# The order of scores, projections and transposes on TensorE in the attention of a hybrid decoder layer

## The chip, the cores and the metric

One NeuronCore of a Trainium2 chip runs the whole layer as one program. The time is that of one execution on the device, in microseconds (us); the kernel before took 1571.97 us, the median of 3 runs from 1569.59 to 1573.26. TensorE multiplies matrices into PSUM, VectorE (DVE), ScalarE (ACT) and GpSimd (POOL) work on tiles, SyncE issues most of the DMAs. Each engine works through its own list of instructions in program order, and semaphores tie the lists together.

## The reference, cut to what matters

One layer for 1024 tokens and a width of 1024: an input projection feeds two kinds of attention, their outputs are gated, merged and projected, and a SwiGLU feed-forward part follows.

```python
qa, ka, va, qb, kb, vb, f_logit, gate_logit = jnp.split(h @ w_in, IN_OFFSETS, axis=-1)

# branch A: 8 query heads, 2 key heads, rotary, a window of 128 keys, a sink per head
s = where(valid, einsum('bnqhgd,bnkhd->bnhgqk', qb_, kb_) * scale, -inf)
p = exp(s - m) / (sum(exp(s - m)) + exp(sink - m));  o_a = p @ v

# branch B: 8 heads, causal over all keys, with the sum of log forget gates
s = einsum('bqhd,bkhd->bhqk', qi, k) * scale + ci - cum_k
p = softmax(where(causal, s, -inf));                 o_b = p @ v

merged = gates[0] * (o_a @ w_branch_a) + gates[1] * (o_b @ w_branch_b)
y = merged @ w_out;  x = x + gate_m * rms_norm(y)
x = x + gate_f * rms_norm((silu(g_part) * u_part) @ w_ffn_out)
```

## The kernel before, in words

Every fp32 product is made of three TensorE products of high and low halves (`TERMS`: hi x hi, hi x lo, lo x hi), so each projection of 512 columns takes 3 x 8 = 24 matmuls, and every operand is split into two halves first.

The attention is one loop of numbered steps (`for gp in range(FIRST, NG)`), written out for each engine separately; the same step numbers run through all of them. Branch A has 16 tiles of 4 heads x 128 queries and takes steps 0 to 31, two groups for each tile. Branch B works on four pairs of heads; the pair `pb` starts at step b = `step0(pb)` = 32, 56, 80, 104 and has 24 groups. Its scores come in eight rows: row r holds 128 queries against (r + 1) x 128 keys for two heads. Steps around the change:

- `scores(r)` on TensorE writes the scores to PSUM. Rows 4 to 7 of a pair use all of the banks 0 to 3, so each waits until DVE has taken the row before (`s_taken`). Which step issues a row stands in `issue_step`: for pairs 2 to 4 rows 0 to 3 in b-11, b-9, b-7, b-5 and rows 4 to 7 in b+1 to b+4; for pair 1 rows 0 to 3 in 25, 27, 27, 28.
- `score_stat(r)` on DVE (L1174 for branch B) adds the forget bias, takes the maximum and writes the row to SBUF (`s_row`). It stands last in DVE's step; in the following step `exps_b` on ACT (L832) makes the exponentials, and two steps after the statistic `denominator` on DVE (L1188) the reciprocal and `normalise` on GpSimd (L674) the probabilities.
- `transpose_p(gp + 1)` on TensorE (L1618, L1624) transposes the 128 x 128 tiles of the next group into bank 4 or 5. It waits for the normalised rows (`norm_ok`) and for the low half of two groups back (`grp_lo`). `group_hi` on ACT (L843) and `group_lo` on DVE (L1193) make the two halves, `group_lo` as the first thing in DVE's step.
- `times_v(gp)` (L1651, L1652) multiplies group gp with the values. The first group of an output waits until DVE has added up the output before (L1200 to L1204).
- `project(j, first, end)` (L1545) makes pieces of the projections that the next pair needs, 4 or 5 matmuls a step in branch B (8 in steps 25 and 27). `fills` says which steps carry which chunk. The second chunk of a pair (steps b+5 to b+10) writes bank 1, so its first piece waits until all eight rows of the pair are taken. In the last pair the pieces belong to the gates, and this chunk starts at b+6.

The loop on TensorE:

```python
            for gp in range(FIRST, NG):
                between = 0 <= gp < 2 * A_T and gp % 2 == 0
                for r in range(N_S):
                    if issue_step[r] == gp and not between:
                        scores(r)
                for j, first, end in mm_at[gp]:
                    project(j, first, end)
                if 0 <= gp + 1 < NG:
                    transpose_p(gp + 1)
                for r in range(N_S):
                    if issue_step[r] == gp and between:
                        scores(r)
                if gp >= 0:
                    times_v(gp)
```

Of the kernel before, what the change touches and what calls it, by code (L numbers as in the profile page):

```python
# [39 lines left out]
def hybrid_layer(nc, x, c, positions, w_ada, b_ada, g_pre_mix, g_post_mix, w_in, b_f, sinks,  # L40
# [165 lines left out]
    A_T, B_P = 2 * NTOK, 4  # L206
    NG = 2 * A_T + B_P * 3 * NTOK
# [25 lines left out]
    def banks(r):  # L233
        is_a, _, i = score_parts(r)
        if is_a:
            return [PS[:, 2 * (r % 2) + kv] for kv in range(2)]
        if i < 4:
            return [PS[:, 2 * (i % 2) + h] for h in range(2)]
        return [PS[:, 2 * h:2 * h + 2].rearrange("p a n -> p (a n)") for h in range(2)]
# [8 lines left out]
    def group_cols(gp):  # L248
        is_a, _, g, _, kb = group_parts(gp)
        if is_a:  # L250
            return 2 * P if g == 0 else NT
        return P * (4 * g + 4 - max(4 * g, kb))
# [100 lines left out]
    with ExitStack() as ctx:  # L353
# [231 lines left out]
        def _(pool):  # L585
# [78 lines left out]
            def normalise(r):  # L664

                is_a, _, i = score_parts(r)
                pool.wait_ge(rden_ok, r + 1)
                if is_a:
                    w = P if i == 0 else 2 * P
                    probs = [p_a[r % 3][:, hd, 0:w] for hd in range(4)]  # L670
                else:
                    probs = [s_row[i][:, h] for h in range(2)]
                for hd, pr in enumerate(probs):
                    ins = pool.tensor_scalar(pr, pr, rden[:, r % 4, hd:hd + 1], 1.0, ALU.mult, ALU.mult)  # L674
                ins.then_inc(norm_ok, 1)
# [741 lines left out]
        def _(pe):  # L1417
# [103 lines left out]
            def project(j, first, end):  # L1521

                n, ch = chunks[j]
                bank = chunk_bank(j)
                if first == 0:
                    pe.wait_ge(w_split, n + 1)
                    if j == 0:
                        pe.wait_ge(h_lo, 2 * KD)
                    elif j in (4, 5, 6):
                        pe.wait_ge(v_taken, 2 * NTOK)  # L1530
                    elif j == 7:
                        pe.wait_ge(cum_taken, CH)
                    elif 8 <= j < 10:
                        pe.wait_ge(proj_taken, j - 1)
                    elif j == 10:
                        pe.wait_ge(proj_taken, 10)
                    elif j > 10 and chunk_bank(j) == 1:
                        pe.wait_ge(s_taken, A_T + NTOK * ((j - 14) // 4 + 1))
                    elif j > N_PROJ:
                        pe.wait_ge(g_done, 1 if j == N_PROJ + 2 else 3)  # L1540
                    elif j > 10:
                        pe.wait_ge(proj_taken, j - 1 if chunk_bank(j - 1) == 1 else j)
                for m in range(first, end):
                    k, (a, b) = m // 3, TERMS[m % 3]
                    ins = nc.tensor.matmul(PS[:, bank], w_hl[a][:, n % 2, k], act_hl[b][:, k, ch * NT:(ch + 1) * NT],  # L1545
                                           start=(m == 0), stop=(m == 3 * KD - 1))
                if end == 3 * KD:
                    ins.then_inc(proj_ready, 1)
# [57 lines left out]
            def transpose_p(gp):  # L1606
                is_a, pb, g, h, kb = group_parts(gp)
                if gp < 2:
                    pe.wait_ge(proj_taken, 5 + gp)
                else:  # L1610
                    pe.wait_ge(grp_lo, gp - 1)
                if is_a:
                    t = gp // 2
                    pe.wait_ge(norm_ok, t + 1)
                    for b in range(1 if g == 0 else 2):
                        for pl in range(2):
                            c = (2 * b + pl) * P
                            ins = nc.tensor.transpose(PS[:, 4 + gp % 2, c:c + P], p_a[t % 3][:, 2 * h + pl, b * P:(b + 1) * P],  # L1618
                                                      ident[:, :])
                else:  # L1620
                    pe.wait_ge(norm_ok, A_T + NTOK * pb + 4 * g + 4)
                    i0 = max(4 * g, kb)
                    for i in range(i0, 4 * g + 4):
                        ins = nc.tensor.transpose(PS[:, 4 + gp % 2, (i - i0) * P:(i - i0 + 1) * P],  # L1624
                                                  s_row[i][:, h, kb * P:(kb + 1) * P], ident[:, :])
                ins.then_inc(grp_ready, 1)

            def times_v(gp):
                is_a, pb, g, h, kb = group_parts(gp)
                n = group_cols(gp)  # L1630
                u = gp // 2 if is_a else A_T + 4 * pb + 2 * g + h
                if (h if is_a else kb) == 0:
                    if u == 0:
                        pe.wait_ge(proj_taken, 9)
                    else:
                        pe.wait_ge(o_taken, u)
                pe.wait_ge(grp_lo, gp + 1)
                p_hi, p_lo = pt_hl[gp % 3]
                if is_a:
                    v = [va_hl[:, max(g - 1, 0) + b, h] for b in range(1 if g == 0 else 2)]  # L1640
                    c0, m = 2 * P * h, 2 * P
                    first, last = True, True
                else:
                    v = [vb_hl[:, kb, 2 * pb + h]]
                    c0, m = NT - n, n
                    first, last = kb == 0, kb == 4 * g + 3
                for b, vv in enumerate(v):
                    both = vv.rearrange("p a d -> p (a d)")
                    cols = slice(b * m, (b + 1) * m)
                    whole = PS[:, 6, c0:c0 + m]  # L1650
                    nc.tensor.matmul(whole, both, p_hi[:, cols], start=first and b == 0, stop=False)  # L1651
                    ins = nc.tensor.matmul(whole, both, p_lo[:, cols], start=False, stop=last and b == len(v) - 1)  # L1652
                ins.then_inc(pv_done, 1)
# [9 lines left out]
            cumulate(1)  # L1663
            project(6, 0, 3 * KD)
            for gp in range(FIRST, NG):
                between = 0 <= gp < 2 * A_T and gp % 2 == 0
                for r in range(N_S):
                    if issue_step[r] == gp and not between:
                        scores(r)
# [9 lines that stand above are left out]
# [195 lines left out]
```

## Time and profile before

| | |
|---|---|
| time, median of 3 runs | 1571.97 us (1569.59 to 1573.26) |
| the profiled execution | 1568.9 us, its span 1567.2 us |
| TensorE matmuls, busy | 1494.8 us, 95% of the span |
| GpSimd, DVE, ACT busy | 631.1, 575.0, 407.6 us |
| L1545 (projections in the loop) | 720 matmuls, 288 us |
| share of TensorE in the chain that ended last | 86% |
| granted TensorE clock, mean | 0.992 |

The attention loop ends at 486 us, and the first transposes of branch B are at 264 us. A row of the timeline reads: start, duration, engine, line, operation, what it writes and reads, shapes, how many alike follow each other, and in brackets the idle time of the engine before it with what ended it. Matmuls overlap; what counts is the distance of their starts.

### The profile page before, as it was taken

The page shows a single profiled execution, that of the slowest core. Times are in us where ns is not written, and L with a number is a line of the kernel's source. Part 1 is how long each engine was busy: PE and PEld are TensorE (multiplying, and loading weights), DVE is VectorE, ACT ScalarE, POOL GpSimd, SP SyncE. Part 2 cuts the span into 40 slices and gives each one's busy share as a digit, 9 for nine tenths or more (in the row PEclk, how much of TensorE's full clock was granted, in tenths as well). Part 3 has the DMA queues.
Part 4 walks back from the last instruction along what each step waited for, and adds up shares of the span by engine and source line. Part 5 has one row for each costly group of instructions (what it writes and reads, how often), then busy time and mean ns, then how long its engine had stood idle before and what let it go on. Part 6 is the DMA issues. An engine that isn't in the chain of part 4 may idle for free.

```text
span 1567.2 us, 18736 instructions
## 1 busy us (share of the span) xinstructions
PE 1494.8 (95%) x7301; PEld 1221.6 (78%) x7301; DVE 575.0 (37%) x912; ACT 407.6 (26%) x834; POOL 631.1 (40%) x512
## 2 busy tenths in 40 slices
PE   4899998989989999999999999999999999999998
PEld 1898776677777888888787888888888887888886
DVE  3776876555544764767553000000000000003002
ACT  3711466555551001002343000000000002433331
POOL 0315734233363534344023332333323334975860
PEclk9999999999999999999999999999999999999999
DMA  9301101021213644333232111111111122434521
GB/s 351 108 14 29 64 25 47 35 68 35 101 55 99 164 135 135 108 108 107 85 117 64 57 40 54 42 52 54 40 54 44 50 67 83 145 108 124 172 95 54
DMA packets 145493, 132.67 MB, mean 85 GB/s; under 512 B 13104, under 2 KB 125832, under 8 KB 144912
## 3 DMA queue, kind: packets, MB, share of 16 engines
q1 hardware_dynamic: 139200, 126.96, 26.1%
q10 hardware_dynamic: 6224, 4.77, 0.9%
q8 instruction: 45, 0.74, 0.2%
q14 instruction: 24, 0.20, 0.0%
HBM read 119.10 MB, written 12.62 MB: 84 GB/s over the span
## 4 chain that ended last, share of the span: by engine, by line
PE 86%; DVE 6%; ACT 3%; POOL 2%; DMA 2%; issue 1%; SPq 0%; ACTq 0%; DVEq 0%; POOLq 0%
PE PS L1421 68%; PE PS L1545 9%; PE PS L1599 2%; DVE s_row L1174 2%; PE PS L1624 2%; PE PS L1651 1%; POOL s_row L674 1%; DMA wada<-in_w_ada_dram 1%; PE PS L1652 1%; PE PS L1432 1%; PE PS L1443 1%; ACT pt_hi L843 1%; DVE pt_lo L1193 1%; DMA w2raw<-in_w_ffn_out_dram 0%; PE PS L1603 0%
## 5 line engine op out<-in xcount | busy, mean ns | idle before, releaser
L1421 PE MATMUL PS<-act_hi,w_hi 128*128 128x512 f32 x928 | 361.9, 390 | 0.0
L1421 PE MATMUL PS<-act_hi,w_lo 128*128 128x512 f32 x928 | 361.1, 389 | 0.0
L1421 PE MATMUL PS<-act_lo,w_hi 128*128 128x512 f32 x928 | 361.1, 389 | 0.0
L634 POOL TENSOR_TENSOR w_lo<-wraw,w_hi 128x1024 fp32r<-128x1024 f32 x81 | 200.3, 2472 | 6.5
L1421 PEld LDWEIGHTS PS<-act_hi,w_lo 128*128 128x128 f32 x928 | 174.2, 188 | 36.3
L1421 PEld LDWEIGHTS PS<-act_lo,w_hi 128*128 128x128 f32 x928 | 174.2, 188 | 36.1
L1421 PEld LDWEIGHTS PS<-act_hi,w_hi 128*128 128x128 f32 x928 | 174.2, 188 | 35.7
L1397 DVE TENSOR_TENSOR act_ff<-PS,sl 128x512 f32 x40 | 27.7, 692 | 407.6 <-PE PS L1421 407.6
L632 POOL CAST w_hi<-wraw 128x1024 fp32r<-128x1024 f32 x81 | 85.9, 1060 | 183.2 <-PE PS L1421 113.0
L1421 PE MATMUL PS<-w_hi,ah_hi 128*128 128x512 f32 x352 | 137.1, 390 | 2.2 <-POOL w_lo L734 2.2
L970 ACT ACTIVATE sl<-PS 128x512 f32<-128x512 f32 x44 | 26.4, 600 | 429.2 <-PE PS L1421 429.2
L1421 PE MATMUL PS<-w_lo,ah_hi 128*128 128x512 f32 x352 | 136.9, 389 | 0.0
L1421 PE MATMUL PS<-w_hi,ah_lo 128*128 128x512 f32 x352 | 136.9, 389 | 0.0
L625 POOL TENSOR_TENSOR scratch<-ones 128x1 f32<-128x1 f32 x44 | 8.9, 203 | 300.0 <-PE PS L1421 293.6
L1193 DVE TENSOR_TENSOR pt_lo<-PS,pt_hi 128x512 fp32r<-128x512 f32 (+3 forms) x128 | 74.4, 582 | 108.8 <-ACT pt_hi L843 108.4
L734 POOL TENSOR_TENSOR w_lo<-w2raw,w_hi 128x1024 fp32r<-128x1024 f32 x44 | 105.5, 2397 | 8.5 <-ACT w_hi L995 8.4
L1545 PE MATMUL PS<-act_hi,w_hi 128*128 128x512 f32 x240 | 96.4, 402 | 3.7 <-DVE qb_lo L1262 1.9
L843 ACT ACTIVATE pt_hi<-PS 128x512 fp32r<-128x512 f32 (+3 forms) x128 | 65.2, 509 | 132.5 <-PE PS L1624 109.6
L674 POOL TENSOR_SCALAR s_row<-s_row,rden 128x128 f32<-128x128 f32 (+7 forms) x64 | 46.9, 746 | 128.7 <-DVE rden L1188 128.5
L1545 PE MATMUL PS<-act_lo,w_hi 128*128 128x512 f32 x240 | 95.9, 400 | 0.0
L1545 PE MATMUL PS<-act_hi,w_lo 128*128 128x512 f32 x240 | 95.7, 399 | 0.0
L731 POOL TENSOR_TENSOR ah_lo<-act_ff,ah_hi 128x512 fp32r<-128x512 f32 x44 | 58.1, 1321 | 62.4 <-ACT ah_hi L993 62.4
(235 smaller groups left out, 2498.8 us busy)
## 6 DMA issues: line engine op xcount, KB each, us to landing
wraw<-in_w_ffn_in_dram SPq DMA_DIRECT2D x44, 512.0 KB
w2raw<-in_w_ffn_out_dram SPq DMA_DIRECT2D x44, 512.0 KB, 3.5
adaraw<-in_w_ada_dram SPq DMA_DIRECT2D x32, 512.0 KB, 3.9
wraw<-in_w_in_dram SPq DMA_DIRECT2D x25, 512.0 KB
wada<-in_w_ada_dram SPq DMA_DIRECT2D x6, 1024.0 KB, 15.1
xin<-in_x_dram SPq DMA_DIRECT2D x8, 512.0 KB, 7.2
cs<-ncum_dram SPq DMA_DIRECT2D x4, 1024.0 KB, 4.7
woraw<-in_w_out_dram SPq DMA_DIRECT2D x8, 512.0 KB, 4.5
```

Source lines behind the costliest of these rows:

```text
L632: pool.tensor_copy(w_hl[0][:, slot], wraw[:, slot]).then_inc(w_hi_ok, 1)
L634: pool.tensor_tensor(w_hl[1][:, slot], wraw[:, slot], w_hl[0][:, slot].bitcast(F32), ALU.subtract)\
L674: ins = pool.tensor_scalar(pr, pr, rden[:, r % 4, hd:hd + 1], 1.0, ALU.mult, ALU.mult)
L731: pool.tensor_tensor(ah_hl[n][1][:, :], act_ff[:, m % FT, cols], ah_hl[n][0][:, :].bitcast(F32), ALU.subtract).then_inc(ah_split, 1)
L734: pool.tensor_tensor(w2_hl[n][1][:, :], w2raw[:, m % 2], w2_hl[n][0][:, :].bitcast(F32), ALU.subtract).then_inc(w2_split, 1)
L843: nc.scalar.activation(pt_hl[gp % 3][0][:, 0:n], PS[:, 4 + gp % 2, 0:n], ACT.Copy).then_inc(grp_hi, 1)
L1174: ins = nc.vector.tensor_tensor_reduce(out=s_row[i][:, h], in0=src[h][:, 0:w], in1=cs[:, h, 0:w], scale=-SM, scalar=BIG, op0=ALU.add, op1= ...
L1193: nc.vector.tensor_tensor(pt_hl[gp % 3][1][:, 0:n], PS[:, 4 + gp % 2, 0:n], pt_hl[gp % 3][0][:, 0:n].bitcast(F32), ALU.subtract).then_inc( ...
L1421: ins = nc.tensor.matmul(out_ap, lhs[a], rhs[b], start=first and i == 0, stop=last and i == 2)
L1545: ins = nc.tensor.matmul(PS[:, bank], w_hl[a][:, n % 2, k], act_hl[b][:, k, ch * NT:(ch + 1) * NT], start=(m == 0), stop=(m == 3 * KD - 1))
L1599: nc.tensor.matmul(dst[h][:, c0:c0 + n], qb_hl[pb % 2][x][rows, i * P:(i + 1) * P], kb_hl[pb % 2][y][rows, c0:c0 + n], start=(e == 0), sto ...
L1624: ins = nc.tensor.transpose(PS[:, 4 + gp % 2, (i - i0) * P:(i - i0 + 1) * P], s_row[i][:, h, kb * P:(kb + 1) * P], ident[:, :])
```

## The change

`between` says whether a step's scores stand ahead of its projections and transposes or behind them. So far it holds for the even steps from 0 to 30; now it holds for every step from 0 on. All scores of branch A from step 0 on are issued in even steps, so it is the rows of branch B that change their place (all but row 3 of the first pair, which is issued in step 28).

```diff
--- before.py
+++ after.py
@@ -1663,7 +1663,7 @@
             cumulate(1)
             project(6, 0, 3 * KD)
             for gp in range(FIRST, NG):
-                between = 0 <= gp < 2 * A_T and gp % 2 == 0
+                between = 0 <= gp < NG
                 for r in range(N_S):
                     if issue_step[r] == gp and not between:
                         scores(r)
```

The first place is step b+1 of the first pair on TensorE. L1599 and L1603 are the scores (the mask is the last of them), L1545 the projection, L1624 the transposes of group b+2, L1651 and L1652 the product with the values. Before, from the mask of row 4:

```order
L1603 MATMUL PS<-maskb,identb 128x128 x2
L1545 MATMUL PS<-act_lo,w_hi 128x512
L1545 MATMUL PS<-act_hi,w_lo 128x512
L1545 MATMUL PS<-act_hi,w_hi 128x512
L1545 MATMUL PS<-act_lo,w_hi 128x512
L1545 MATMUL PS<-act_hi,w_lo 128x512
L1624 MATMUL PS<-ident,s_row_125 128x128
L1624 MATMUL PS<-ident,s_row_126 128x128
L1651 MATMUL PS<-pt_hi_117,vb_hl 128x384
L1652 MATMUL PS<-pt_lo_118,vb_hl 128x384
```

Now, from the start of the step:

```order
L1545 MATMUL PS<-act_lo,w_hi 128x512
L1545 MATMUL PS<-act_hi,w_lo 128x512
L1545 MATMUL PS<-act_hi,w_hi 128x512
L1545 MATMUL PS<-act_lo,w_hi 128x512
L1545 MATMUL PS<-act_hi,w_lo 128x512
L1624 MATMUL PS<-ident,s_row_125 128x128
L1624 MATMUL PS<-ident,s_row_126 128x128
L1599 MATMUL PS<-kb_hi_104,qb_hi_108 128x512 x2
L1599 MATMUL PS<-kb_lo_105,qb_hi_108 128x512 x2
L1599 MATMUL PS<-kb_hi_104,qb_lo_109 128x512 x2
```

The five projection matmuls and the two transposes stand in front of the scores of row 4, and the product with the values follows the scores directly.

The second place is the same pair's step b+4 on TensorE, from the end of the scores of row 7 to the first projection matmul of step b+5. Before:

```order
L1603 MATMUL PS<-maskb,identb 128x128 x2
L1545 MATMUL PS<-act_lo,w_hi 128x512
L1545 MATMUL PS<-act_hi,w_lo 128x512
L1545 MATMUL PS<-act_hi,w_hi 128x512
L1545 MATMUL PS<-act_lo,w_hi 128x512
L1545 MATMUL PS<-act_hi,w_lo 128x512
L1624 MATMUL PS<-ident,s_row_124 128x128
L1624 MATMUL PS<-ident,s_row_125 128x128
L1624 MATMUL PS<-ident,s_row_126 128x128
L1651 MATMUL PS<-pt_hi_117,vb_hl 128x512
L1652 MATMUL PS<-pt_lo_118,vb_hl 128x512
L1545 MATMUL PS<-act_hi,w_hi 128x512
```

Now, from the last matmuls of row 7:

```order
L1599 MATMUL PS<-kb_hi_104,qb_lo_109 128x512 x2
L1599 MATMUL PS<-kb_hi_104,qb_hi_108 128x512 x2
L1599 MATMUL PS<-kb_lo_105,qb_hi_108 128x512 x2
L1599 MATMUL PS<-kb_hi_104,qb_lo_109 128x512 x2
L1603 MATMUL PS<-maskb,identb 128x128 x2
L1651 MATMUL PS<-pt_hi_117,vb_hl 128x512
L1652 MATMUL PS<-pt_lo_118,vb_hl 128x512
L1545 MATMUL PS<-act_hi,w_hi 128x512
```

Between row 7 and the projection of the next step only the product with the values is left; the five projection matmuls and the three transposes are ahead of row 7. On DVE, ACT and GpSimd no instruction changes its place.

## Rows read from the trace of the kernel before

**Rows 1.** The page, first part: busy time, share of the span and instructions of TensorE.
```profile
PE 1494.8 (95%) x7301; PEld 1221.6 (78%) x7301; DVE 575.0 (37%) x912; ACT 407.6 (26%) x834; POOL 631.1 (40%) x512
```

**Rows 2.** Waits of TensorE, 240 to 490 us: total us, times, longest us.
```profile
PE PS L1624 <- POOL s_row L674: 4.7, 5, 1.0
PE PS L1599 <- DVE nm L1174: 4.5, 9, 0.7
...
PE PS L1651 <- DVE ostage L1201: 3.7, 4, 1.7
PE PS L1651 <- DVE ostage L1204: 3.4, 7, 0.6
PE PS L1545 <- DVE nm L1174: 1.7, 3, 0.6
```

**Rows 3.** Timeline of TensorE, pair 1, step b+1: start us, us, instruction, [idle before].
```profile
270.12 0.48 PE L1545 MATMUL PS<-act_lo,w_hi 128*128 128x512 f32 x1
...
271.50 0.42 PE L1651 MATMUL PS<-pt_hi,vb_hl 128*128 128x384 f32 x1
...
272.07 0.50 PE L1599 MATMUL PS<-kb_hi,qb_hi 64*128 64x512 f32 x2
```

**Rows 4.** Timeline of TensorE, pair 1, from P(b+4) to T(b+8).
```profile
281.30 0.48 PE L1545 MATMUL PS<-act_lo,w_hi 128*128 128x512 f32 x1
...
284.05 0.47 PE L1545 MATMUL PS<-act_hi,w_hi 128*128 128x512 f32 x1 [0.56 <-DVE nm L1174]
...
287.09 0.38 PE L1651 MATMUL PS<-pt_hi,vb_hl 128*128 128x256 f32 x1 [0.29 <-DVE pt_lo L1193]
...
289.56 0.63 PE L1624 MATMUL PS<-ident,s_row 128*128 128x128 f32 x4 [1.04 <-POOL s_row L674]
```

**Rows 5.** Timeline of VectorE and GpSimd, pair 1, steps b+1 to b+5.
```profile
270.35 0.82 DVE L1174 CUSTOM_DVE_ANT_0 s_row<-PS,cs 128x640 f32<-128x640 f32 x1 [0.86 <-PE PS L1603]
...
281.53 1.22 DVE L1174 CUSTOM_DVE_ANT_0 s_row<-PS,cs 128x1024 f32<-128x1024 f32 x1 [0.49 <-PE PS L1603]
...
284.89 0.15 DVE L1188 RECIPROCAL rden<-den 128x2 f32<-128x2 f32 x1
...
285.14 4.28 POOL L674 TENSOR_SCALAR s_row<-s_row,rden 128x896 f32<-128x896 f32 x4 [2.22 <-DVE rden L1188]
```

**Rows 6.** Timeline of TensorE, pair 4, step b+1: P(b+1) and V(b+1).
```profile
436.52 0.47 PE L1545 MATMUL PS<-act_lo,w_hi 128*128 128x512 f32 x1
...
437.66 0.42 PE L1651 MATMUL PS<-pt_hi,vb_hl 128*128 128x384 f32 x1
```

**Rows 7.** Timeline: V(26), then in step 51 and 52 the statistic and V.
```profile
249.23 0.39 PE L1651 MATMUL PS<-pt_hi,va_hl 128*128 128x256 f32 x1 [1.46 <-DVE ostage L1201]
...
313.72 0.69 DVE L1174 CUSTOM_DVE_ANT_0 s_row<-PS,cs 128x512 f32<-128x512 f32 x1
...
315.09 0.48 PE L1651 MATMUL PS<-pt_hi,vb_hl 128*128 128x512 f32 x1
...
317.04 0.48 PE L1651 MATMUL PS<-pt_hi,vb_hl 128*128 128x512 f32 x1
```

**Rows 8.** Windows: us, busy of each engine, PEclk (granted clock); two projection matmuls.
```profile
257.40:261.50 4.10, 1.34 (x10) 0.94 (x8) 2.46 (x9) 4.04 (x13) 2.24 (x5) 1.00 0.61 155
262.00:268.00 6.00, 5.14 (x19) 4.38 (x20) 2.69 (x6) 1.38 (x4) 1.36 (x2) 0.50 0.07 22
284.00:289.50 5.50, 4.18 (x19) 2.99 (x19) 1.83 (x6) 2.86 (x7) 4.22 (x4) 1.00 0.50 194
452.30:456.00 3.70, 1.66 (x9) 0.97 (x7) 0.79 (x3) 2.74 (x6) 3.04 (x4) 1.00 0.62 180
456.10:459.50 3.40, 3.40 (x13) 2.91 (x13) 1.39 (x2) 1.19 (x2) 3.31 (x3) 0.50 1.05 256
...
266.25 0.63 PE L1545 MATMUL PS<-act_lo,w_hi 128*128 128x512 f32 x1
...
266.68 0.63 PE L1545 MATMUL PS<-act_hi,w_lo 128*128 128x512 f32 x1
```

## The prediction, made before the changed kernel was run

> **Names.** S(r) are the scores of row r of a pair of heads of the second branch (r = 0 to 7), P(n), T(n) and V(n) the projection matmuls, the transposes of group n and the product with the values of group n. Steps are counted from a pair's first step b, as b+1. The four pairs are called 1 to 4.
>
> **What bounds the kernel now.** I read the page's engine line first: TensorE is busy for 95% of the span [rows 1], so every microsecond that it idles, and that nothing else pays back, is in the time. Then the waits of TensorE from 240 to 490 us, where the moved scores are [rows 2]. Two lines matter: S waits for DVE's row statistic nine times, 4.5 us, and the first transposes of a group wait for GpSimd's normalised rows five times, 4.7 us. Then the timeline of pair 1 in both directions. S(4) is issued until 270.12, S(5) starts at 272.07; rows 4 to 7 share all four score banks, so each waits until DVE has taken the one before. DVE sits idle 0.86 us before the statistic of row 4 and 0.49 us before that of row 7, both times released by the last instruction of the scores [rows 3, 5]. So TensorE's scores and DVE's statistics alternate: from S(4) on this is a chain in which neither has slack. Behind it stand, in DVE's program order, the low half of one group, the low half of a projection and the reciprocal of row 6 (284.89), then GpSimd's 4.28 us on rows 6 and 7, and only then T(b+8), at 289.56 after 1.04 us of idling [rows 4, 5]. What fills TensorE meanwhile are P, T and V, which can't run out of it: it idles 0.56 us before P(b+5) too, which writes a bank that row 7 used.
>
> **What the change removes, adds and moves.** Nothing is added or removed; on DVE, ACT and GpSimd no instruction moves. On TensorE, S moves behind P and T of its own step in 31 places: rows 0, 1, 2 of pair 1 (steps 25, 27, 27), rows 4 to 7 of all four pairs (steps b+1 to b+4), rows 0 to 3 of pairs 2 to 4 (b-11, b-9, b-7, b-5). The order shows P, then T, then S, then V: what changed is S against P and T, while P and T keep their order. All other scores of the first branch stood like this already.
>
> *Rows 4 to 7, pairs 1 to 3.* S(4) now has P(b+1) and T(b+2) in front of it. These take from 270.12 to 271.50 in the trace, 1.38 us: five matmuls at 0.23 us and two transposes [rows 3]. S(4) ends 1.38 us later, and the statistic of row 4 with it, since DVE was waiting. From there each gap between two scores holds V, P and T in place of P, T and V: nearly the same work, still shorter than the statistic plus its hand-over (S(5) to S(7) already waited). So S(7) and its statistic are 1.38 us late too. Behind S(7), TensorE now has V(b+4) alone until P(b+5), which waits for that statistic; P(b+4) and T(b+5), which filled the 2.75 us from 281.30 to 284.05 [rows 4], have been used up in front. The idle time before P(b+5) grows from 0.56 to about 1.9 us. Behind that point everything is as before, T(b+8) still waiting 1.04 us for GpSimd. Loss: 3 x 1.38 = 4.1 us. The work put in front is not lost work; it is the cover of the chain, spent before the chain starts.
>
> *Pair 4.* Here a step has four projection matmuls: from 436.52 to 437.66, 1.14 us [rows 6]. P(b+5) doesn't wait for row 7 there, but V(b+5) waits for the low half that DVE makes after row 7's statistic, and T(b+8) for GpSimd. Loss 1.1 us.
>
> *Rows 0 to 3, pairs 2 to 4.* Nobody waits for these rows for several steps, but DVE's statistic stands in front of the low half of the next group. Of row 3: S(3) would end where V(51) starts; the statistic of 1.3 us started at 313.72 before, now at about 315.2, and with the low half (0.7 us) it is done at 317.3; V(52) began at 317.04 [rows 7]. That is +0.3 us each, 0.9 for three pairs. Rows 0 to 2 have shorter statistics and later needs; I take nothing for them. The other end: none of it shows, 0.
>
> *Rows 0 to 2 of pair 1.* The same mechanism in two steps of longer projections (eight matmuls, 8 x 0.23 = 1.9 us). By the nearest row, that of row 3, up to 0.3 us each, down to nothing where V waits anyway, as V(26) does at 249.23 [rows 7]; I take 0.2 for both.
>
> *Early transposes.* A transpose needs the low half of two groups back, and its normalised row, and has both in every moved step. ACT's copies come earlier, DVE's low halves don't, for they stand behind the statistic. What could be gained at most are the waits of V that follow moved steps: V(26), 1.46 us [rows 7], and three of the seven for L1204, 0.5 each by their mean [rows 2]. I take 0.
>
> Sum: 4.1 + 1.1 + 0.9 + 0.2 = 6.3 us. The profiled execution took 1568.9 us (span 1567.2 and 1.7 around it), so 1575.2 for it; the median of the three runs lies 3.1 us above it at 1571.97, and there the sum gives 1578.3.
>
> **The clock.** TensorE was granted half its clock (0.50, the 1.2 GHz level) from 262 to 268 us, after 4.1 us in which it had been busy for 1.34, and from 456.1 to 459.5, after 3.7 us with 1.66 busy; from 284 to 289.5 us, behind the chain of pair 1, it was busy 4.18 of 5.5 us and kept 1.00 [rows 8]. At half clock the matmuls of P stand 0.43 us apart (266.25 and 266.68) against 0.23, so 3.4 us of it cost 3.4 x (1 - 0.23/0.43) = 1.6 us. The new gap of 1.9 us before P(b+5) thins exactly the place that so far kept the full clock. Most of such a fall would be hidden, as T(b+8) waits 1.04 us there and V(b+6) 0.29; outside that cover it costs the full 1.6 us.
> The Trainium skill, "TensorE: Matmul & The Clock Gate", section "HAM oscillation — how this bites in real kernels", says that a kernel whose bursts of matmuls alternate with waits gets its clock taken down again and again, and pays with half of the throttled time. By that rule the three pairs would each fall once; the trace agrees that it happens in this kernel after a sparse stretch, and no row shows whether 1.9 us is enough.
>
> **The rivals.**
> *Clock falls at the new gaps.* For: rows 8. Against: the cover named. Three falls outside the cover: 6.3 + 3 x 1.6 = 11.1 us, 1583. The same mechanism can also work backwards: if the two falls of before land elsewhere, 3.2 us less than forecast, 1575.
> *The chain has slack.* If GpSimd's start were not tied to row 7, the delay would vanish in the 0.56 + 0.29 + 1.04 us that TensorE idles anyway in each pair, and only the small terms stay: +1.1, 1573.1, no change. Against it: DVE's reciprocal of row 6 stands behind the statistic of row 7 in program order, and nothing in [rows 5] reports DVE idle between the two.
> *Faster.* The copies by ACT and the low halves come early enough for V to stop waiting in the moved steps: -(1.5 + 3 x 0.5) = -3.0 us, 1569.0. It decides only if the slack rival holds as well, that is if S(5) starts no later than now; one lost P and T per pair outweighs it. Against it, the low half can't pass the statistic on DVE.
> *The change does something else than its words.* Had the scores gone between T and P, only the transposes (0.1 us of the 1.38) would stand in front of S(4), and nothing would be measured. The order on TensorE excludes this.
>
> **How the numbers follow.** Forecast (+6.3) 0.61; more than two clock falls' worth above it 0.19; slack 0.14; faster 0.06. A change of 0.2%, 3.1 us, is about what can be told from none. Forecast and clock are slower; of the slack case a quarter would be by its other terms; the faster case may end within the bound. That makes slower 0.83, same 0.12, faster 0.05. The range: from below, falls that land better (-3.2) and medians that scatter by 1.8 give 1573; from above, 1583 and the scatter give 1584. The likeliest is 1578.3.
>
> **What would show it.** In the profile after: S(4) of pair 1 behind P and T, 1.4 us later after the start of its step; DVE's idle time before that statistic up from 0.86 to over 2 us; TensorE's wait of P(b+5) for the statistic up from 1.7 us in three to about 5.8 in three; the waits of S for the statistic near 4.5 and of T for GpSimd near 4.7 as before; V(b+5) of pair 4 waiting about 1.2 us for a low half where it waited for nothing; all stages after 490 us as long as before. I am wrong if P(b+5) waits as long as before, if T(b+8) stops waiting for GpSimd, or if the waits of V shrink by more than those of P grow.

## The result, and the profile after

The changed kernel took 1576.89 us, the median of 15 runs (1574.89 to 1581.42); the kernel before took 1573.08 us beside it, also 15 runs (1569.36 to 1575.41). The ratio is 1.003 with a 95% interval of 1.002 to 1.0041, so the change costs 3.1 to 6.4 us (the two medians alone lie 3.8 us apart). The profiled execution took 1575.0 us with a span of 1573.3, 6.1 us more than that of before. The forecast was 6.3 us more.

First the page's engine line of the changed kernel, the answer to [rows 1], and the waits of TensorE from 240 to 495 us, the answer to [rows 2]:

```profile
PE 1499.5 (95%) x7301; PEld 1226.5 (78%) x7301; DVE 573.2 (36%) x912; ACT 408.9 (26%) x834; POOL 632.7 (40%) x512
```

```profile
PE PS L1545 <- DVE nm L1174: 6.1, 3, 2.0
PE PS L1651 <- DVE pt_lo L1193: 4.5, 4, 1.7
PE PS L1651 <- DVE ostage L1201: 3.6, 4, 1.7
PE PS L1651 <- DVE ostage L1204: 3.4, 7, 0.6
PE PS L1599 <- DVE nm L1174: 3.1, 6, 0.8
PE PS L1624 <- POOL s_row L674: 1.9, 3, 1.0
```

TensorE does the same work. The wait of the projections for the row statistic went from 1.7 to 6.1 us, in the same three places. The wait of the transposes for GpSimd went the other way, from 4.7 to 1.9; why, the clock below tells. The scores wait 1.4 us less, yet counted from S(4) they start no earlier: S(5) comes 3.23 us behind S(4), before 3.24. A larger part of each gap is filled.

The timeline of TensorE in pair 1, the answer to [rows 3, 4]: first the start of S(4) in the kernel before, then in the changed kernel the starts of P(b+1), S(4), V(b+1), S(5), then V(b+4), which now follows S(7), P(b+5) and T(b+8).

```profile
268.83 0.50 PE L1599 MATMUL PS<-kb_hi,qb_hi 64*128 64x512 f32 x2
```

```profile
267.92 0.40 PE L1545 MATMUL PS<-act_lo,w_hi 128*128 128x512 f32 x1
...
269.39 0.50 PE L1599 MATMUL PS<-kb_hi,qb_hi 64*128 64x512 f32 x2
...
270.67 0.42 PE L1651 MATMUL PS<-pt_hi,vb_hl 128*128 128x384 f32 x1
...
272.62 0.50 PE L1599 MATMUL PS<-kb_hi,qb_hi 64*128 64x512 f32 x2
...
281.87 0.47 PE L1651 MATMUL PS<-pt_hi,vb_hl 128*128 128x512 f32 x1
...
284.62 0.76 PE L1545 MATMUL PS<-act_hi,w_hi 128*128 128x512 f32 x1 [2.04 <-DVE nm L1174]
...
290.50 0.63 PE L1624 MATMUL PS<-ident,s_row 128*128 128x128 f32 x4 [0.37 <-POOL s_row L674]
```

P(b+1) now takes the place of S(4) right behind V(b), and S(4) comes 1.47 us behind it. From the start of S(4) to P(b+5) it takes 15.23 us, before 15.22 (268.83 to 284.05): the chain itself has not changed. It starts later, and its cover, P(b+4) and T(b+5), the work that TensorE used to do while DVE was busy with row 7, is no longer behind S(7): 2.04 us of idling where there were 0.56.

VectorE and GpSimd in the same stretch, the answer to [rows 5]: the statistic of row 4, that of row 7, the reciprocal of row 6, and GpSimd on row 6 and row 7.

```profile
270.90 0.82 DVE L1174 CUSTOM_DVE_ANT_0 s_row<-PS,cs 128x640 f32<-128x640 f32 x1 [2.22 <-PE PS L1603]
...
282.10 1.22 DVE L1174 CUSTOM_DVE_ANT_0 s_row<-PS,cs 128x1024 f32<-128x1024 f32 x1 [0.79 <-PE PS L1603]
...
285.46 0.15 DVE L1188 RECIPROCAL rden<-den 128x2 f32<-128x2 f32 x1
...
285.70 2.01 POOL L674 TENSOR_SCALAR s_row<-s_row,rden 128x896 f32<-128x896 f32 x2 [2.52 <-DVE rden L1188]
...
288.13 2.22 POOL L674 TENSOR_SCALAR s_row<-s_row,rden 128x1024 f32<-128x1024 f32 x2 [0.42 <-DVE rden L1188]
```

DVE idles 2.22 us before the first statistic (0.86 before). From there to the reciprocal of row 6 it takes 14.56 us, before 14.54. Only GpSimd's row 7 comes later than it should, 2.43 us behind row 6 where it followed without a break: its reciprocal stands behind the low half of a group whose transposes were slowed, as the clock rows below show.

Pair 4, the answer to [rows 6], and for row 3 of pair 2 the first half of its statistic, the low half that stands behind it, V(51) and V(52), the answer to [rows 7]:

```profile
456.78 0.44 PE L1651 MATMUL PS<-pt_hi,vb_hl 128*128 128x384 f32 x1 [1.28 <-DVE pt_lo L1193]
...
316.25 0.69 DVE L1174 CUSTOM_DVE_ANT_0 s_row<-PS,cs 128x512 f32<-128x512 f32 x1 [1.50 <-PE PS L1603]
...
317.47 0.69 DVE L1193 TENSOR_TENSOR pt_lo<-PS,pt_hi 128x512 fp32r<-128x512 f32 x1
...
316.02 0.48 PE L1651 MATMUL PS<-pt_hi,vb_hl 128*128 128x512 f32 x1
...
318.21 0.50 PE L1651 MATMUL PS<-pt_hi,vb_hl 128*128 128x512 f32 x1
```

V(b+5) of pair 4 waits 1.28 us, where it waited for nothing. V(52) starts 2.19 us behind V(51), before 1.95 (315.09 to 317.04): the low half that it needs follows the statistic without a break and ends at 318.16, 0.05 us before V(52).

The clock, the answer to [rows 8]: windows of the changed kernel (start and end, busy time of each engine, the third number from the right is TensorE's granted clock).

```profile
282.70:284.60 1.90, 0.00 (x0) 0.01 (x1) 1.90 (x5) 0.63 (x3) 0.49 (x1) 1.00 0.00 0
284.70:288.00 3.30, 3.30 (x10) 2.71 (x11) 1.37 (x5) 2.56 (x5) 2.01 (x2) 0.50 0.76 308
342.80:346.00 3.20, 3.20 (x11) 2.61 (x10) 0.88 (x4) 1.92 (x5) 2.67 (x3) 0.50 0.89 328
400.80:404.00 3.20, 3.20 (x11) 2.63 (x10) 0.79 (x3) 1.41 (x4) 3.14 (x4) 0.50 0.99 408
462.20:465.40 3.20, 3.20 (x13) 2.71 (x12) 1.39 (x2) 1.19 (x2) 3.11 (x3) 0.50 1.06 259
```

A low-clock stretch of the 1.2 GHz level begins behind each of the three new gaps, the first after 1.90 us in which TensorE did nothing; the profile of before has none of the three. (The last window stands behind T(b+8) of pair 4, where the kernel before had a low-clock stretch too, from 456.1 in [rows 8].) P, T and V behind the gap are slower, and T(b+8) then finds its row ready or nearly so: it idles 0.37, 0 and 0 us instead of 1.04, 1.04 and 1.05. That is where the 2.8 us that vanished from the wait for GpSimd are: what was idling is now spent in slow matmuls.

### The profile page after: what moved, and what is told of

The parts are those of the page before. It is cut to its first block, busy times and chain, and to the rows that moved or that the text cites. A ratio compares the mean times of both kernels' runs of the same rounds, so it can differ in the third digit from the quotient of the medians.

```text
span 1573.3 us, 18736 instructions
## 1 busy us (share of the span) xinstructions
PE 1499.5 (95%) x7301; PEld 1226.5 (78%) x7301; DVE 573.2 (36%) x912; ACT 408.9 (26%) x834; POOL 632.7 (40%) x512
## 4 chain that ended last, share of the span: by engine, by line
PE 87%; DVE 6%; ACT 3%; issue 2%; DMA 2%; POOL 1%; SPq 0%; DVEq 0%; ACTq 0%; POOLq 0%
PE PS L1421 67%; PE PS L1545 10%; PE PS L1599 2%; PE PS L1624 2%; PE PS L1651 2%; DVE s_row L1174 1%; PE PS L1652 1%; DMA wada<-in_w_ada_dram 1%; PE PS L1432 1%; PE PS L1443 1%; DVE pt_lo L1193 1%; POOL s_row L674 1%; ACT pt_hi L843 1%; DMA w2raw<-in_w_ffn_out_dram 0%; PE PS L1603 0%
## 5 line engine op out<-in xcount | busy, mean ns | idle before, releaser
L1421 PE MATMUL PS<-act_hi,w_hi 128*128 128x512 f32 x928 | 361.9, 390 | 0.0
L1421 PE MATMUL PS<-act_hi,w_lo 128*128 128x512 f32 x928 | 361.1, 389 | 0.0
L1421 PE MATMUL PS<-act_lo,w_hi 128*128 128x512 f32 x928 | 361.1, 389 | 0.0
L1421 PEld LDWEIGHTS PS<-act_lo,w_hi 128*128 128x128 f32 x928 | 174.3, 188 | 36.1
L1421 PEld LDWEIGHTS PS<-act_hi,w_lo 128*128 128x128 f32 x928 | 174.2, 188 | 36.1
L1421 PEld LDWEIGHTS PS<-act_hi,w_hi 128*128 128x128 f32 x928 | 174.3, 188 | 35.8
L1421 PE MATMUL PS<-w_hi,ah_hi 128*128 128x512 f32 x352 | 137.1, 390 | 2.4 <-POOL w_lo L734 2.4
L1421 PE MATMUL PS<-w_lo,ah_hi 128*128 128x512 f32 x352 | 137.0, 389 | 0.0
L1421 PE MATMUL PS<-w_hi,ah_lo 128*128 128x512 f32 x352 | 136.9, 389 | 0.0
L1545 PE MATMUL PS<-act_hi,w_hi 128*128 128x512 f32 x240 | 97.4, 406 | 8.1 <-DVE nm L1174 6.1
L1545 PE MATMUL PS<-act_hi,w_lo 128*128 128x512 f32 x240 | 96.2, 401 | 0.0
L1545 PE MATMUL PS<-act_lo,w_hi 128*128 128x512 f32 x240 | 96.2, 401 | 0.0
```

The source lines that it names most:

```text
L1421: ins = nc.tensor.matmul(out_ap, lhs[a], rhs[b], start=first and i == 0, stop=last and i == 2)
```

## The experiments

Distances in the timeline of TensorE, one profiled execution of each kernel, say more than the times, which scatter by 5 us. Two of them are used: *chain*, from the start of V(b) to the start of T(b+8), and *rest*, from there to the next pair's V(b).

| kernel | chain, pairs 1, 2, 3, 4 | rest, three times | ratio to before [95%] |
|---|---|---|---|
| before | 21.54, 21.40, 21.39, 21.38 | 34.10, 34.06, 34.09 | 1 |
| changed | 23.28, 22.79, 22.77, 22.54 | 34.43, 34.44, 34.46 | 1.0030 [1.0020, 1.0041] |
| e1, rows 4 to 7 only | 22.80, 23.14, 22.79, 22.54 | 34.11, 34.09, 34.11 | 1.0039 [1.0026, 1.0052] |
| e2, rows 0 to 3 only | 21.72, 21.39, 21.39, 21.41 | 34.44, 34.46, 34.47 | 1.0004 [0.9995, 1.0013] |
| e3, T first, then S, P, V | 21.64, 21.62, 21.61, 21.61 | 33.68, 33.68, 33.61 | 0.9989 [0.9979, 0.9998] |
| e4, rows 4 to 7 a step earlier | 19.57, 19.57, 19.59, 18.91 | 35.27, 35.26, 35.28 | 0.9985 [0.9977, 0.9994] |
| e5, changed, with filler | 23.09, 22.76, 22.76, 22.53 | 34.45, 34.44, 34.44 | 1.0026 [1.0017, 1.0034] |
| e6, row 4 only | 23.01, 22.78, 22.76, 22.52 | 34.08, 34.06, 34.13 | 1.0033 [1.0021, 1.0045] |
| e7, row 7 only | 22.40, 22.40, 22.39, 21.92 | 34.11, 34.07, 34.11 | 1.0024 [1.0014, 1.0034] |
| e8, e3 and e4 together | 19.55, 19.59, 19.59, 18.92 | 34.81, 34.81, 34.81 | 0.9955 [0.9942, 0.9968] |
| e8 once more | 19.55, 19.56, 19.58, 18.90 | 34.86, 34.87, 34.85 | 0.9982 [0.9973, 0.9991] |
| e9, a copy between | 19.55, 19.54, 19.56, 18.27 | 34.84, 34.86, 34.84 | 0.9964 [0.9950, 0.9977] |

In e4, e8 and e9 the scores of row 4 lie in front of V(b), so 1.2 us of the chain are counted in the rest; there only the sum of both compares. Pair 1 compares less well than the others: a low-clock stretch ends close to its V(b) in every profile (at 268.4 us before, where V(b) starts at 268.02), and where it ends moves the chain of pair 1 by up to 0.3 us.

Behind T(b+8) of pair 4 the loop runs out in 31.81 us in the kernel before and in the changed one and in 31.89 in e1, to the first matmul of the branch projections (L1421); in all other versions in 30.99 to 31.13. The three longer ones have a low-clock stretch there (from about 456.1, 462.2 and 463.4 us), the others do not. So about 0.8 us of any difference between the profile of before and those of e2 to e9 belongs to the clock in pair 4.

### e1 and e2: which of the moved scores cost

```diff
e1                 between = 0 <= gp < 2 * A_T and gp % 2 == 0
+                between = between or gp >= 2 * A_T and 1 <= (gp - 2 * A_T) % (3 * NTOK) <= 4
e2 -                between = 0 <= gp < 2 * A_T and gp % 2 == 0
+                between = 0 <= gp < NG
+                if gp >= 2 * A_T and 1 <= (gp - 2 * A_T) % (3 * NTOK) <= 4:
+                    between = False
```

> Of the 31 moved scores only rows 4 to 7 of the four pairs are moved (16 of them); rows 0 to 3 stay in front of their projections. Chain theory (the projection and the transposes put in front of S(4) are the loss): P(b+1) and T(b+2) by the trace of before, 3 x 1.38 + 1.14 = 5.3 us slower than before in the profile, ratio about 1.003, nearly all of the change. The wait of P(b+5) for the statistic 6 us in three, as in the changed kernel. Rival, spread loss (each of the 31 moved scores costs a little, because DVE's low half comes later or TensorE switches differently): about half of it, 16 of 31, 2.4 us. Rival, clock alone: the three low-clock stretches behind the gaps show here too; if they are the loss, the distance from S(4)'s step start to T(b+8) grows by more than the 1.38 us.

> The other half: rows 0 to 3 of pairs 2 to 4 and rows 0 to 2 of pair 1 are moved behind projection and transposes (15 scores), rows 4 to 7 stay. Chain theory: nobody waits for these rows, about 0.3 us for row 3 of each of three pairs and 0.2 for pair 1, +1.1 us at most, ratio 1.0000 to 1.0007; no low-clock stretch near 284, 342 and 400 us. Spread loss: +2.3 us.

e1 is as slow as the changed kernel, by the ratio and by the chain; its rest is that of before. e2 can't be told from before by its time; its chain is that of before (0.18 us longer in pair 1), and its rest is 0.34 to 0.40 us longer, as in the changed kernel. The two halves add up to the whole, and the loss isn't spread over the 31 scores. The waits of TensorE for the statistic, first in e1, then in e2:

```profile
PE PS L1545 <- DVE nm L1174: 6.1, 3, 2.0
PE PS L1599 <- DVE nm L1174: 3.1, 6, 0.8
```

```profile
PE PS L1599 <- DVE nm L1174: 4.4, 9, 0.7
PE PS L1545 <- DVE nm L1174: 1.7, 3, 0.6
```

6.1 us before the projections in the one, 1.7 as before in the other. In e1 low-clock stretches fell into pair 2, from 343.9 us, where the chain is 0.35 us longer than in the changed kernel, and into pair 3, from 401.9, where it isn't; in pair 1 none followed its gap of 2.04 us, and T(b+8) waited 1.07 us as before.

### e6 and e7: the first link alone, the last alone

```diff
-                between = 0 <= gp < 2 * A_T and gp % 2 == 0
e6 +                between = between or gp >= 2 * A_T and (gp - 2 * A_T) % (3 * NTOK) == 1
e7 +                between = between or gp >= 2 * A_T and (gp - 2 * A_T) % (3 * NTOK) == 4
```

(`between` keeps its old value first in both.)

> Only row 4 of each pair (4 of the 31 scores) is moved behind P(b+1) and T(b+2); rows 5 to 7 stay in front. Chain theory: what counts is what stands in front of the first link, so the whole loss of rows 4 to 7 is here, 22.8 us from V(b) to T(b+8) in pairs 2 and 3 (before 21.4) and +5.3 us in all, ratio 1.003 to 1.004. The gap appears between S(4) and S(5) (about 1.2 us), not in front of P(b+5). Rival, each moved score costs its share: a quarter of it, +1.3 us.

> Only row 7 of each pair is moved behind P(b+4) and T(b+5), the last link. Chain theory: before, row 7 waited about 0.5 us for DVE (0.7 in pair 4); P and T take 1.48 us (pair 4 1.26), so S(7) starts 1.0 us later (0.6), and everything behind it with it: 22.4 us from V(b) to T(b+8) in pairs 2 and 3, +3.6 us in all, ratio 1.002. Rival, quarter share: +1.3 us. Moved together (the changed kernel) the two don't add up to 5.3 + 3.6, since the delay of the first link covers that of the last.

One moved score in each pair, 4 of 31, makes the whole loss of the 16: the chain is 22.78 and 22.76 us. In e6's timeline the gap stands before S(5), and P(b+5) and T(b+8) wait as before:

```profile
271.42 0.50 PE L1599 MATMUL PS<-kb_hi,qb_hi 64*128 64x512 f32 x2
...
274.65 0.51 PE L1599 MATMUL PS<-kb_hi,qb_hi 64*128 64x512 f32 x2 [1.35 <-DVE nm L1174]
...
286.66 0.47 PE L1545 MATMUL PS<-act_hi,w_hi 128*128 128x512 f32 x1 [0.56 <-DVE nm L1174]
...
292.19 0.63 PE L1624 MATMUL PS<-ident,s_row 128*128 128x128 f32 x4 [1.05 <-POOL s_row L674]
```

In e7 S(7) no longer waits for DVE, since P and T in front of it take the 0.47 us that it used to wait and 1.0 us more, and the gap is before P(b+5):

```profile
282.13 0.50 PE L1599 MATMUL PS<-kb_hi,qb_hi 64*128 64x512 f32 x2
...
286.57 0.47 PE L1545 MATMUL PS<-act_hi,w_hi 128*128 128x512 f32 x1 [2.04 <-DVE nm L1174]
```

The chain is 22.40 and 22.39 us in pairs 2 and 3, expected were 22.4; pair 4 gave +0.54. So work put in front of a link costs its own length minus what that link waited anyway, and the delays don't add: e6 and e7 together would make 2.4 us in pair 2, the changed kernel has 1.39. The place of the idle gap doesn't matter: e6 has it before S(5), e1 before P(b+5), at nearly the same cost.

### e5: the clock

The extra matmuls write to a PSUM bank that the next transposes overwrite; the wait keeps them off data still in use.

```diff
+                if gp in [step0(pb) + 5 for pb in range(B_P - 1)]:
+                    pe.wait_ge(grp_lo, gp)
+                    for _ in range(8):
+                        nc.tensor.matmul(PS[:, 4 + (gp + 1) % 2], act_hl[0][:, 0, 0:P],
+                                         act_hl[0][:, 0, 0:NT], start=True, stop=True)
                 for j, first, end in mm_at[gp]:
```

> The changed kernel, and in pairs 1 to 3 eight extra matmuls of 512 columns, whose results nobody reads, in the new gap in front of P(b+5) (8 x 0.23 = 1.9 us of a gap of 2.0 us). In the changed kernel's profile a low-clock stretch of 3.4 us starts at each of these gaps (284.6, 342.7, 400.7 us). Clock theory (part of the loss is the clock): no low-clock stretch there, and from V(b) to T(b+8) a pair takes less than the 23.28, 22.79 and 22.77 us of the changed kernel; at most 0.4 us in pair 1. Chain theory with hidden falls: the stretches go, T(b+8) waits 1.0 us for GpSimd again in pairs 1 to 3 where it waited 0.37, 0 and 0, and pairs 2 and 3 stay at 22.8 us; the time as the changed kernel's, ratio to before about 1.003.

```profile
284.04 2.02 PE L1673 MATMUL PS<-act_hi 128*128 128x512 f32 x8
...
286.25 0.47 PE L1545 MATMUL PS<-act_hi,w_hi 128*128 128x512 f32 x1 [0.19 <-DVE nm L1174]
...
291.77 0.63 PE L1624 MATMUL PS<-ident,s_row 128*128 128x128 f32 x4 [1.05 <-POOL s_row L674]
```

```profile
286.30:291.70 5.40, 4.15 (x19) 2.91 (x19) 1.73 (x6) 2.76 (x6) 4.24 (x4) 1.00 0.52 196
```

With the filler (L1673) in the gap the clock stays at 1.00, T(b+8) waits 1.05 us for GpSimd again in all pairs, and the chain is no shorter in pairs 2 and 3. In pair 1, P(b+5) to T(b+8) takes 5.52 us, before 5.51 (284.05 to 289.56), in the changed kernel 5.88 (284.62 to 290.50). So in these profiles the falls of the clock cost 0.36 us in pair 1 and 0.03 and 0.01 in pairs 2 and 3; the idle time in front of T(b+8) hid the rest. (The whole chain of pair 1 is only 0.19 us shorter than in the changed kernel, because its part up to P(b+5) is 0.17 longer, 17.57 against 17.40, next to the low-clock stretch at V(b).)

### e3: the transposes first

```diff
+                moved = gp >= 0 and not between and gp in issue_step
+                if moved and gp + 1 < NG:
+                    transpose_p(gp + 1)
                 for r in range(N_S):
                     if issue_step[r] == gp and not between:
                         scores(r)
                 for j, first, end in mm_at[gp]:
                     project(j, first, end)
-                if 0 <= gp + 1 < NG:
+                if 0 <= gp + 1 < NG and not moved:
                     transpose_p(gp + 1)
```

> In the 31 places the transposes of the next group go first, then the scores, then the projection, then the product with the values; the other steps as before. Chain theory: only T(b+2) stands in front of S(4), two transposes of 0.07 us each by their distance in the trace, so +0.14 us per pair, ratio 1.000 (0.999 to 1.001); the wait of P(b+5) back near 0.6 us each. Rival, early transposes (what is bad is that the transposes move ahead of the scores): as slow as the changed kernel, +4 to +6 us. Rival, gain: the waits of V for low halves shrink, up to 3 us faster.

Here the transposes stand before the scores as in the changed kernel, but not the projection, and the loss is gone: the chain is 0.1 us longer than before in pair 1 and 0.22 in the others. So it is the projection ahead of S(4) that cost. The rest is 0.4 us *shorter*: the early transposes, which the prediction gave nothing, win where no chain is held. The wait of V(48) for an output, 0.42 us, and those of V(72) and V(96), 0.43 each, are gone; one of 0.55 at V(b+8) of pair 4 is new, in the place where before had its low clock. The row of before, and the total of that wait in e3 (before 3.4 us in seven):

```profile
308.02 0.50 PE L1651 MATMUL PS<-pt_hi,vb_hl 128*128 128x512 f32 x1 [0.42 <-DVE ostage L1204]
...
PE PS L1651 <- DVE ostage L1204: 2.6, 5, 0.6
```

In all it is 0.1% faster than before; the interval barely excludes no change.

### e4: the chain one step earlier

```diff
-        rows += [b + 1, b + 2, b + 3, b + 4]
+        rows += [b, b + 1, b + 2, b + 3]
```

> The other direction: the order in a step is as before, but rows 4 to 7 of each pair, their statistics, exponentials and normalising are done one step earlier on all engines (steps b to b+3 in place of b+1 to b+4). Chain theory: S(4) starts earlier by P(b), T(b+1) and V(b), 1.9 to 2.2 us; TensorE idles 0.56 + 0.29 + 1.04 us per pair behind the chain, so up to 1.9 us per pair can be won: 4 to 7.5 us faster than before, ratio 0.995 to 0.9975, and T(b+8) no longer waits for GpSimd. Rival (the chain isn't what TensorE waits for): no change, the waits of T(b+8) stay near 1.0 us or turn into waits of V.

The direction was right, the size was not: 2.4 us (0.15%) where 4 to 7.5 were expected. Chain and rest together take 54.84 us, before 55.64, 55.46 and 55.48: 0.6 to 0.8 per pair, not 1.9. (From T(32) to the first matmul of the branch projections, pair 4 included, it is 219.38 us, 4.3 less than before, 0.8 of them the clock in pair 4.) Where did the rest go? TensorE, ACT and GpSimd behind row 7 in pair 1:

```profile
285.80 0.50 PE L1651 MATMUL PS<-pt_hi,vb_hl 128*128 128x512 f32 x1 [0.32 <-DVE ostage L1204]
...
288.46 0.44 PE L1651 MATMUL PS<-pt_hi,vb_hl 128*128 128x384 f32 x1 [0.78 <-DVE pt_lo L1193]
...
291.56 0.63 PE L1624 MATMUL PS<-ident,s_row 128*128 128x128 f32 x4 [0.28 <-POOL s_row L674]
...
284.93 1.14 ACT L832 ACTIVATE s_row<-s_row,nm 128x1024 f32<-128x1024 f32 x1
...
286.06 1.15 ACT L832 ACTIVATE s_row<-s_row,nm 128x1024 f32<-128x1024 f32 x1
...
287.32 0.49 ACT L843 ACTIVATE pt_hi<-PS 128x384 fp32r<-128x384 f32 x1
...
289.19 2.23 POOL L674 TENSOR_SCALAR s_row<-s_row,rden 128x1024 f32<-128x1024 f32 x2 [1.27 <-DVE rden L1188]
```

P(b+5) waits no more, and T(b+8) only 0.28 us. But V(b+4) now waits 0.32 for an output and V(b+5) 0.78 for a low half, whose copy on ACT (287.32) stands behind the two exponentials of row 7 (from 284.93). The old 0.29 us wait of V(b+6) has moved up a step with the row and grown. It holds GpSimd too: before, GpSimd went through rows 6 and 7 without a break (4.28 us [rows 5]), now it idles 1.27 us before row 7, whose reciprocal on DVE (288.94) stands behind this late low half (287.84) and the low half of a projection.

### e8 and e9: both gains, and a try at the new wait

e8 is e4 with e3's order in the steps of rows 0 to 3. e9 adds on ACT:

```diff
                 for h in range(2):
+                    if i == 7 and h == 1:
+                        group_hi(s_step[r] + 2)
                     ins = nc.scalar.activation(s_row[i][:, h], ...
```

and leaves this copy out at its old place.

> A version meant to be faster than both: rows 4 to 7 and their statistics, exponentials and normalising one step earlier with the scores first in the step, and in the steps of rows 0 to 3 the transposes first, then scores, projection, values. Chain theory: the gains of the two kernels measured so far add up, as they lie in different stretches: -0.7 us per pair from the early chain and -0.4 us from T(b+8) to the next V(b) for each of three pairs, 4 us in all, ratio 0.997 to 0.998. Rival: what the transposes give in steps b-11 to b-5 is the same idle time as the chain's, then no better than 0.9985.

> The kernel of e8_both once more, on the same chip as its variant: ratio to before 0.9955 to 0.997, 19.6 us from V(b) to T(b+8) in pairs 1 to 3 and 34.8 us from there to the next V(b).

> The kernel with rows 4 to 7 a step earlier and early transposes, and on ACT the high half of group b+5 stands between the exponentials of the two heads of row 7 instead of behind both. There V(b+5) waited 0.78 us for the low half that follows this copy, and V(b+4) 0.32 us. Theory (what the earlier chain couldn't win is a wait behind row 7's exponentials on ACT): the wait of V(b+5) shrinks to 0.3 us or less, and each pair takes 0.3 to 0.8 us less from V(b) to T(b+8) as far as GpSimd, which gets row 7 a copy (0.5 us) later, allows it: T(b+8) then waits longer than 0.3 us; 1 to 2 us faster in all. Rival: the time until T(b+8) is set by GpSimd's normalising of rows 6 and 7 in any case; then the wait only moves from V(b+5) to T(b+8), and a pair stays at 19.6 us or is up to 0.5 us slower.

e8 is the fastest version: chain and rest take 54.40 us in pair 2, 1.06 less than before. The gains add up: e4 has 0.63 there, and the rest of e3 0.38. Its ratio came out as 0.9955 and as 0.9982 in two measurements whose intervals don't meet; 0.997 to 0.998 were expected of the first and 0.9955 to 0.997 of the second, and neither hit, while the distances in the pairs agree to 0.06 us. In the two profiled executions (1568.3 and 1572.0 us) V(b) of pair 1 starts at 269.78 and at 274.58 us, so these two differ by 4.8 us ahead of the pairs and hardly in them; the granted clock was 0.50 from 261.6 to 268.2 us in the one and from 264.4 to 274.4 in the other. What the medians owe to this isn't shown. The gain is 0.2 to 0.45%. In e9 the rival was right for pairs 1 to 3:

```profile
287.17 0.38 PE L1653 MATMUL PS<-pt_hi,vb_hl 128*128 128x256 f32 x1 [0.39 <-DVE pt_lo L1195]
...
289.25 0.63 PE L1626 MATMUL PS<-ident,s_row 128*128 128x128 f32 x4 [0.65 <-POOL s_row L674]
...
286.89 2.21 POOL L674 TENSOR_SCALAR s_row<-s_row,rden 128x1024 f32<-128x1024 f32 x2 [1.24 <-DVE rden L1190]
...
286.03 0.69 DVE L1264 TENSOR_TENSOR kb_lo<-PS,kb_hi 128x512 fp32r<-128x512 f32 x1 [1.05 <-ACT kb_hi L891]
```

V(b+5) waits no more (V(b+6) 0.39), T(b+8) waits 0.65 instead of 0.28, the chain stays 19.55. T(b+8) waits for GpSimd's row 7, but GpSimd isn't what is late: it idles 1.24 us before row 7 for DVE's reciprocal. That stands behind the low half of a projection (286.03, the last row), which waits 1.05 us for its high half on ACT, and this copy still stands behind the exponentials of row 7. So the end is set by ACT's exponentials and what DVE has queued in front of the reciprocal; moving that low half behind the reciprocal was not tried. Only in pair 4, where T(b+8) had no wait, the chain is 0.65 us shorter. The time of e9 against e8 in the same measurement, 1566.1 against 1568.8 us, is more than the loop explains; where the other 2 us come from isn't shown.

## Why the prediction was right

The direction, the size and the main mechanism came out as forecast. Two of its signs did not. The wait of the transposes for GpSimd fell from 4.7 to 1.9 us, and in pairs 2 and 3 T(b+8) stopped waiting for GpSimd, which the prediction had named as a sign of being wrong: that is the clock (below), and it cost 0.37 us in all. And the scores wait 3.1 us for the statistic in place of 4.5, since a larger part of the gaps is filled.

- *The chain from S(4), and P and T ahead of it (3 x 1.38).* Right, shown by e1, e6 and e3. Pairs 2 and 3 gave 1.39 and 1.38. Pair 1 gave 1.74: 1.37 up to P(b+5), and 0.37 behind it by the clock (e5), which the sum had at nothing.
- *Pair 4 (1.14).* 1.16; the wait of V(b+5) is 1.28 us, forecast 1.2.
- *Rows 0 to 3 (0.3 a pair).* 0.33, 0.38 and 0.37, and e2 has the same without the rest of the change (0.34, 0.40, 0.38).
- *Pair 1's rows 0 to 2 (0.2).* Not seen: V(26) waits 1.31 instead of 1.46 us, and the stretch from the first scores of branch A to T(32) is no longer (110.01 us, before 110.22).
- *Early transposes (0).* In the changed kernel nothing. But e3 shows 0.4 us per pair from early transposes alone. The prediction's reason, that the low halves stand behind the statistic and so come no earlier, doesn't hold there: in e3 the statistic hardly moves, in the changed kernel the projection in front of the scores delays it. That this delay is what ate the gain is argued from the order, not measured apart.
- *The clock.* Three falls at the three gaps, and the prediction's own remark held that most of such a fall would be hidden: T(b+8) and V(b+6) had 1.04 and 0.29 us of idle time to give, a fall was put at 1.6, and the price was 0.37, 0 and 0. But the sum went on with T(b+8) waiting 1.04 us: it waits 0.37, 0 and 0. The Trainium skill ("TensorE: Matmul & The Clock Gate", "HAM oscillation — how this bites in real kernels") tells of falls in a kernel whose TensorE waits about 3 to 5 us at a time for its DMAs. The gaps here are 2.04 us, shorter than that, so the prediction read more into the Trainium skill than stands there when it took a fall for each pair from it; the trace shows that the shorter gaps can do it, in three of three pairs here and in three of six in e1 and e7. Nor does the price that the Trainium skill gives there, half of the throttled time, hold here: the stretches behind these gaps are over 3 us long and cost 0.37 us at most, because the slow matmuls lay where TensorE would have idled; the one in pair 4 costs about 0.8.
- *The sum.* 6.3 us forecast, 6.1 between the two profiled executions, 6.8 over the stretch from T(32) to the first matmul of the branch projections (223.70 and 230.46 us). The four chains give 5.67 of the 6.8 and the three rests 1.08. That the forecast meets them so closely is in part luck: the 0.37 us of the clock, forecast 0, stand against the 0.2 of pair 1's early rows, forecast and not seen. And the 6.1 is 6.8 less 0.8 that the changed kernel's execution was ahead at T(32) (263.28 against 264.09 us), 0.6 of it before the first scores (153.27 against 153.87), where both run the same instructions, and plus 0.2 behind the loop. The ratio of all runs gives 4.7, from 3.1 to 6.4. The forecast lies at the upper end of that interval, and 1578.3 us lies 1.4 above the measured median. (The upper end of the range should be 1584.9, from 1571.97 + 11.1 + 1.8, not 1584; nothing hangs on it.) Both profiles are of quick executions: 1568.9 us is below all 15 runs of the kernel before, and only four of the changed kernel's 15 took 1575.01 us or less. What makes the middle of the runs differ less than the two profiles isn't shown. One source of scatter can be seen: in some profiles low-clock stretches stand far behind the loop, where both profiles compared here have none until TensorE has finished. From the first branch matmul to the end the kernel before takes 1079.4 us, the changed one 1079.6, e3 1083.1 and e2 1085.3, though all four run the same instructions there. The row of before and that of e2 for the same stretch of time:

```profile
1334.00:1340.00 6.00, 6.00 (x28) 4.99 (x27) 0.00 (x0) 3.16 (x4) 5.99 (x5) 1.00 0.45 119
```

```profile
1334.00:1340.00 6.00, 5.72 (x14) 4.55 (x15) 0.00 (x0) 1.58 (x2) 6.00 (x5) 0.50 0.37 131
```

- *The rivals.* *The chain has slack* fell with e6, where the delay of one link came through entirely. *Faster* fell; its gain exists only apart from the projection's move (e3). *Clock falls at the new gaps*: the mechanism is there, but its price was 0.4 us in place of 3 x 1.6.

## What to carry to other kernels

Look for a chain in which two engines wait for each other in turn, and see what stands in front of its first link. Independent work behind a link fills time in which the engine would wait anyway; the same work in front of the first link delays the whole chain by its full length, here 1.38 us a pair. So a move that adds no instruction can slow an engine that is busy for 95% of the time: its filling work is spent before the chain starts and is missing where the engine waits. And moving a chain earlier pays only until something else sets its end, here ACT's exponentials and the work that DVE has queued in front of the reciprocal (e4, e8, e9).

## What the runs showed of the hardware

TensorE's granted clock fell to 0.50 behind idle gaps of 2.04 us in an otherwise busy stretch, in three of three pairs of the changed kernel, in two of three in e1 and in one of three in e7, with the same gap each time; with eight filler matmuls in the gap (e5) it fell in none. So such a gap is enough, but does not always do it. In pair 4 it fell behind shorter gaps: in the kernel before at 456.0 us, after waits of 1.00 us (at 453.51) and 1.04 us (at 455.98). In e3 the same two waits brought no fall. A fall can be free: in pairs 2 and 3 of the changed kernel the clock stood at 0.50 for over 3 us and the chain was 0.03 and 0.01 us longer than with the filler. Low-clock stretches also stand in the long projection stages near 850 and 1335 us in some kernels' profiles and not in others that run the same instructions there.
